# Value columns computed token by token in a mLSTM / SSD / retention step, and three changed orders on ScalarE and VectorE

## The reference, cut to what matters

```
p = rmsnorm(x) @ w_in
# layer 0: q, k, v, gates, og, z, xbc, dt = split(p)     mLSTM, 4 heads of 256 value columns, beside SSD
# layer 1: q, k, v, g = split(p)                         retention, 8 heads of 256 value columns
s = (q @ k^T) * decay ;  out = s @ v + (q @ state) ;  state = decay * state + (k * g)^T @ v
```

## Time and profile before

| | before |
|---|---|
| median of 3 runs | 1037.89 us (1037.03 to 1038.46) |
| the profiled execution, its own time | 1032.65 us |
| its span in the profile | 1030.9 us |
| TensorE busy, share of the span | 991.7 us, 96% |
| VectorE busy | 747.9 us, 73% |
| ScalarE busy | 559.2 us, 54% |
| GpSimd busy | 381.0 us, 37% |
| mean granted TensorE clock | 0.984 |

### The profile page before, as it was taken

The page is one execution under the profiler, slowest core; times in us unless marked ns, Lnnn a source line. Parts: engine busy times, 40 slices in busy tenths (PEclk is TensorE's granted clock), DMA queues, the critical chain, the costliest instruction groups (busy, mean ns, idle before and its releaser), DMA issues.

```text
span 1030.9 us, 19172 instructions
## 1 busy us (share of the span) xinstructions
PE 991.7 (96%) x7256; PEld 939.5 (91%) x7256; DVE 747.9 (73%) x1326; ACT 559.2 (54%) x932; POOL 381.0 (37%) x599
## 2 busy tenths in 40 slices
PE   7989999898899999999999999999999999999996
PEld 6989888777589999999999999899989999999996
DVE  5776788877866999996458857677765699999442
ACT  6536666633544766555444356666645566665431
POOL 4003223224211777772005521322222377777100
PEclk9999999999899999999999999999999999999998
DMA  8463464453555554545444735776635455544541
GB/s 295 140 242 123 129 210 131 153 187 108 168 180 185 173 175 165 164 164 180 163 164 164 266 126 189 219 236 183 206 133 187 161 172 170 169 166 165 179 144 46
DMA packets 64684, 177.22 MB, mean 172 GB/s; under 512 B 5888, under 2 KB 24064, under 8 KB 64592
## 3 DMA queue, kind: packets, MB, share of 16 engines
q1 hardware_dynamic: 64304, 174.86, 51.0%
q0 software_dynamic: 288, 1.12, 0.3%
HBM read 154.92 MB, written 21.05 MB: 171 GB/s over the span
## 4 chain that ended last, share of the span: by engine, by line
PE 85%; DVE 6%; ACT 4%; issue 3%; POOL 1%; DMA 1%; SPq 0%; DVEq 0%; ACTq 0%; POOLq 0%
PE bank L809 25%; PE bank L811 24%; PE bank L810 24%; PE bank L855 2%; ACT wh L1227 2%; DVE wl L1633 1%; PE bank L1165 1%; PE bank L1133 1%; DMA raw<-wts 1%; PE bank L1095 1%; PE bank L867 1%; POOL sts L2353 1%; PE bank L876 1%; PE bank L875 0%; PE bank L1139 0%
## 5 line engine op out<-in xcount | busy, mean ns | idle before, releaser
L1227 ACT ACTIVATE wh<-raw 128x1024 fp32r<-128x1024 f32 x257 | 270.5, 1057 | 318.3 <-PE bank L811 317.6
L1633 DVE TENSOR_TENSOR wl<-raw,wh 128x1024 fp32r<-128x1024 f32 x257 | 321.3, 1254 | 164.4 <-ACT wh L1227 162.4
L809 PE MATMUL bank<-hH,wh 128*128 128x288 f32 x1160 | 352.9, 304 | 7.1 <-DVE wl L1633 4.8
L810 PE MATMUL bank<-hL,wh 128*128 128x288 f32 x1160 | 345.5, 298 | 0.0
L811 PE MATMUL bank<-hH,wl 128*128 128x288 f32 x1160 | 344.3, 297 | 0.0
L809 PEld LDWEIGHTS bank<-hH,wh 128*128 128x128 f32 x1160 | 221.0, 191 | 10.7 <-DVE wl L1633 3.4
L810 PEld LDWEIGHTS bank<-hL,wh 128*128 128x128 f32 x1160 | 221.2, 191 | 0.6
L811 PEld LDWEIGHTS bank<-hH,wl 128*128 128x128 f32 x1160 | 221.5, 191 | 0.0
L1756 DVE SCALAR_TENSOR_TENSOR cy<-pad,vec,cy 128x304 f32<-128x304 f32 (+1 forms) x212 | 139.5, 659 | 4.5 <-ACT cy L1275 0.6
L2194 POOL COPY pad<-fst 128x16 f32<-128x16 f32 x88 | 94.3, 1076 | 67.7 <-DVE cy L1756 67.7
L809 PE MATMUL bank<-upH,wh 128*128 128x288 f32 x352 | 104.4, 297 | 0.0
(11 more groups left out here) (336 smaller groups left out, 1605.7 us busy)
## 6 DMA issues: line engine op xcount, KB each, us to landing
raw<-wts SPq DMA_DIRECT2D x257, 512.0 KB, 3.3
st<-r_in SPq DMA_DIRECT2D x9, 512.0 KB, 6.5
r_out<-st SPq DMA_DIRECT2D x9, 512.0 KB, 4.4
st<-c_in SPq DMA_DIRECT2D x8, 514.0 KB, 6.8
c_out<-st SPq DMA_DIRECT2D x8, 514.0 KB, 5.0
sts<-h_in SPq DMA_DIRECT2D x12, 256.0 KB, 5.1
h_out<-sts SPq DMA_DIRECT2D x12, 256.0 KB, 2.6
st3r<-r_in SPq DMA_DIRECT2D x4, 512.0 KB, 6.0
```

Source lines behind the costliest of these rows:

```text
L809: mm(out, h, xh, start=(k == 0), stop=False)
L810: mm(out, h, xl, start=False, stop=False)
L1227: s.do(act(wh[:, c % RING, :], raw[:, c % RING, :], ACT.Copy), hi_ready)
L1633: do(tt(wl[:, c % RING, :], raw[:, c % RING, :], wh[:, c % RING, :].bitcast(F32), ALU.subtract), lo_ready)
```

## The change

The change has two parts. The first gives the value columns another form. Two value tiles become one pair of 256 columns. The tokens are now stationary and the weights move: `value_half` issues, for each of eight K steps, six matmuls for the prompt (two blocks of 128 tokens, three products each, 256 weight columns moving) and two for the samples, whose high and low halves lie side by side as 64 stationary columns (`xsA`, `xsR`, made by ScalarE's `side_by_side`). The pair fills two tile banks, and TensorE claims both at its start. VectorE's `values` writes the token-major result directly, scaled by `rcol`, a column of inverse norms, which comes from one transpose of `rstd` per layer (`rc0`, `rc2`) and `row_columns`. The transposes of the value tiles and the copies behind them are gone. On the host, `ordered` puts the blocks of a pair in the order in which they are read.

The second changes three orders. `gate_exponentials` and `gate_slab` come two tiles later. ScalarE's `keys` comes before its step for tile t + 3, and before `inverse`, in both kinds of head. In the a-heads VectorE does the taps of tile t + 1 after the sample read-out and the updates, no longer before them.

```diff
@@ plan_banks, layer 1
         tile(group_tile(h, 0))
+        if turns_left:
+            tile(group_tile(h, 1))
         job(f"roi{h}", "act", "five")
...
@@ TensorE
+            def value_half(n, t, xs):
+                half, c = TILES[t][2] % 2, place(t, 0)[0]
+                if half == 0:
+                    claim(t)
+                    claim(t + 1)
+                    pe.wait_ge(xs_ready, n + 2)
+                out, smps, x = mb(t - half), mb(t - half + 1), operand_of(n)
+                pe.wait_ge(lo_ready, c + 1)
+                for i in range(4):
+                    k = 4 * half + i
+                    (xh, xl), w = x(k), slice(2 * i * P, 2 * (i + 1) * P)
+                    h, lo = wh[:, c % RING, w], wl[:, c % RING, w]
+                    for g in range(2):
+                        tok, to = slice(g * P, (g + 1) * P), out[:, g * AV:(g + 1) * AV]
+                        mm(to, xh[:, tok], h, start=(k == 0 and g == 0), stop=False)
+                        mm(to, xl[:, tok], h, start=False, stop=False)
+                        mm(to, xh[:, tok], lo, start=False, stop=(k == KD - 1 and g == 1))
+                    mm(smps[0:2 * NS, 0:AV], xs[:, k, :], h, start=(k == 0), stop=False)
+                    last = mm(smps[0:2 * NS, 0:AV], xs[:, k, :], lo, start=False, stop=(k == KD - 1))
+                last.then_inc(gemm_done, 1)
...
-                if t - 1 in VALUE:
-                    n = VALUE.index(t - 1)
-                    wait_tile_empty(pe, t - 1)
-                    turn(f"v{n}", vT[:, n % 2, :])
+                if t == RCOL["even"]:
+                    pe.wait_ge(rstd_ready, 1)
+                    turn("rc0", rstd)
@@ ScalarE
-                if t == GATES + 4:
+                if t == GATES + 6:
                     gate_exponentials()
...
                 product(f"asp{h}", pout[:, h % 2, 0:AV + 1])
-                step_a(t + 3)
                 if h + 1 < AH:
                     keys("a", h + 1, h + 1)
+                step_a(t + 3)
...
                     s.do(act(vst[row, 0:CV], rvA[0:NS, h, 2, :], ACT.Copy), vst_hi)
+                if h + 1 < CH:
+                    keys("r", h + 1, hg + 1)
                 step(h, 3)
                 if h:
                     inverse(hg - 1)
-                if h + 1 < CH:
-                    keys("r", h + 1, hg + 1)
@@ VectorE
+            def values(t, dst):
+                wait_tile(eng, t)
+                for g in range(2):
+                    do(ts(dst(g), mb(t - 1)[:, g * AV:(g + 1) * AV], rcol[:, g:g + 1], None, ALU.mult), gemm_dve if g else None)
+                b = mb(t)
+                do(ts(dst(2)[0:NS], b[NS:2 * NS, 0:AV], rcol[NS:2 * NS, 2:3], None, ALU.mult))
+                settle()
+                do(stt(out=dst(2)[0:NS], in0=b[0:NS, 0:AV], scalar=rcol[0:NS, 2:3], in1=dst(2)[0:NS],
+                       op0=ALU.mult, op1=ALU.add), gemm_dve)
...
-                if t == GATES + 5:
+                if t == GATES + 7:
                     gate_slab()
...
+                if t == RCOL["even"] + 1:
+                    row_columns("rc0")
...
-                step_a(t + 3)
+                step_a(t + 3, taps=False)
                 sample_out_a(h)
                 updates_a(h, range(4))
+                taps_of(t + 1)
```

More of the change, by code:

```diff
@@ L189, in plan_banks @@
             job("norm0", "act", "five")
[L190 to L191 removed]
+        if t == RCOL["even"]:
+            job("rc0", "dve", "five")
     for h in range(AH):
@@ L268, in plan_banks @@
             late_states(job, h - 1, "five")
-        tile(group_tile(h, 1))
-        if turns_left:
-            job(f"rv{2 * h + 2}", "dve", "five")
+        if not turns_left:
+            tile(group_tile(h, 1))
         job(f"ro1{h}", "act", "five")
@@ L297 @@
 GATES = START["even"] + EVEN.index(("gates", 0))
+RV = [START["odd"] + ODD.index(("rv", i)) for i in range(2 * CH)]
+RCOL = {"even": START["even"] + 5, "odd": START["odd"] + 4}
 def group_tile(h, step):
@@ L392, in build @@
         rstd = keep.take("rstd", [P, T])
+        rcol = keep.take("rcol", [P, 4])
         conv = Area(keep.at)
@@ L977, in _ @@
                     row_max(2)
-                tiles([t], operand_of(0))
+                if t in VALUE:
+                    value_half(0, t, xsA)
+                else:
+                    tiles([t], operand_of(0))
                 if t == T0 + 2:
@@ L1171, in group @@
                 t = group_tile(h, step)
-                if t < START["odd_out"]:
+                if t in RV:
+                    value_half(2, t, xsR)
+                elif t < START["odd_out"]:
                     tiles([t], operand_of(2))
@@ L1180, in _ @@
             for t in range(O + 2, O + LEAD):
-                tiles([t], operand_of(2))
+                if t in RV:
+                    value_half(2, t, xsR)
+                else:
+                    tiles([t], operand_of(2))
+                if t == RCOL["odd"]:
+                    pe.wait_ge(rstd_ready, 3)
+                    turn("rc2", rstd)
                 if t == O + LEAD - 2:
                     front("r", 0, qk_r)
-                    turn_value(0)
-            turn_value(1)
             for h in range(CH):
@@ L1275, in first_tap, with side_by_side @@
                 s.do(act(cy[:, n % 4, 0:width], x[:, 0:width], ACT.Identity, scale=tap, bias=bias), tap_done)
+            def side_by_side(n, xs):
+                eng.wait_ge(xlo_ready, KD * (n + 1))
+                for i in range(2):
+                    s.do(act(xs[:, :, i * NS:(i + 1) * NS], H[n][i][:, :, TP:T].bitcast(F32), ACT.Copy), xs_ready)
             def y_high(n, dst, src):
@@ L1575, in _ @@
                 split(last_chunk(t) + 3)
+                if t == O + 3:
+                    side_by_side(2, xsR)
             eng.wait_ge(rope_ready, 2 * CH)
@@ L1882, in _, with step_a @@
             eng.wait_ge(zeroed, 1)
-            def step_a(t):
+            def step_a(t, taps=True):
                 if t - 1 == GATES:
@@ L2088, in evacuate_odd @@
                 elif kind == "rv":
-                    scaled(t, rvT[:, i % 2, :])
+                    if i % 2:
+                        values(t, lambda g: rvA[:, i // 2, g, :])
                 else:
@@ L2119, in _ @@
                 split(last_chunk(t) + 3)
+                if t == RCOL["odd"] + 1:
+                    row_columns("rc2")
             front("r", 0, AH)
-            value(0)
             for h in range(CH):
@@ L2124, in _ @@
                 step(h, 0)
-                if h == 0:
-                    value(1)
-                else:
+                if h:
                     sample_out(h - 1)
@@ L2462, in halves, with ordered @@
         return weight_tiles(w).reshape(-1, 4, 2, CHUNK, P, P).swapaxes(1, 2).reshape(-1, P, P)
-    def ordered(w, tiles):
-        return weight_tiles(w).reshape(len(tiles), KD, P, P)[tiles].reshape(-1, P, P)
+    def ordered(w, tiles, values):
+        out = weight_tiles(w).reshape(len(tiles), KD, P, P)[tiles]
+        for n in values:
+            out[n:n + 2] = out[n:n + 2].swapaxes(0, 1).reshape(2, KD, P, P).copy()
+        return out.reshape(-1, P, P)
     odd_first = {"rq": 0, "rk": CH, "rv": 2 * CH, "rg": 4 * CH}
```

58 lines of the change are left out of this document (27 added, 31 removed).

## The result

The changed kernel takes 1057.9 us (median of 4 runs, 1057.68 to 1059.64) beside 1037.46 us for the kernel before: ratio 1.0206, 95% interval 1.0185 to 1.0227, or 20 us more. The forecast was 1049.3 us in a range of 1037 to 1060: the direction and the range held, and the size was 8.6 us short, so that the time lies above the 1043 to 1056 of the likeliest case. The profiled execution took 1059.64 us (span 1057.9).

What follows compares the result with a forecast made beforehand. TensorE was taken to bound from 345 to 540 us and in the r-heads, with waits and lower clock from 98 to 345 us. Terms 13.8 - 5.9 + 0 - 8 + 9 + 2.5 = +11.4 gave 1049.3 us, range 1037 to 1060.

Steps and rivals of the forecast that it cites:

- likeliest case: Whole kernel: the forecast sum holds, with its own range of 1043 to 1056 us; chance 0.62.
- Value matmuls, +13.8: Value tiles of both layers: a pair's K step goes from 0.800 to 0.944 us, +13.8 us over 12 pairs x 8 steps.
- load-bound rival: Value matmuls: each keeps 0.133 us because loading the stationary operand sets the pace; +23.2, 1061 us; chance 0.11.
- Transposes, -5.9: Value tiles: 24 value transposes go, less two new ones for `rc0` and `rc2`; -5.9 us.
- The whole value part, 7.9: Value tiles: the matmul term of +13.8 us and the transpose term of -5.9 us taken together.
- Gates, 0: Gates: two waits go, but a new 3.6 us wait at tile 9 for tile 7's bank comes; 0, bounds -3.5 and +2.
- A-heads, -8: A-heads: waits for `keys` and the read-out, with lower clock behind them, mostly go; -8 us, bounds -12 and -4.
- the prediction's own sign: A-heads: the prediction is wrong if they lose less than 4 or more than 12 us.
- R-heads, +9: R-heads 1 to 6: `back` newly waits 1.5 us each for VectorE's `normalise`; +9 us, bounds 0 and 11.
- Clock, +2.5: At the new waits: 1.5 losses of 1.7 us each to lower clock; +2.5 us, bounds 0 and 12.
- that the wait does not come: Rival, r-heads: ScalarE's late split is absorbed, so no new wait; +0.9, 1038.8 us; chance 0.17.
- The faster one: Rival, 98 to 345 us: relief of VectorE lets 22 us go, not 8; -2.6, 1035.3 us; chance 0.08.

Runs made afterwards that it cites:

- e3: The changed kernel with `keys` of the r-heads moved back behind the split and `inverse`; 1041.35 us, ratio 1.0062 to the kernel before.
- e10: The changed kernel with r-heads' `keys` behind `inverse`, `gate_logs` one tile later and `rcol` at the top of memory; 1035.09 us, ratio 1.0017 to the kernel before.
- e11: The kernel before with the changed orders of the gates and a-heads, taps moved last, no r-heads order or new value matmuls; 1025.38 us, ratio 0.9927.
- e6: The kernel before with the gates' order and a-heads' `keys` ahead of the split, taps left in place; 1026.12 us, ratio 0.9893.
- e4: The changed kernel with the taps of the a-heads back ahead of the split; 1059.03 us, ratio 1.0219 to the kernel before.
- e9: The changed kernel with `gate_logs` one tile later, behind the evacuation of tile 7; 1053.98 us, ratio 1.0216 to the kernel before.
- e5: The kernel before with only `rcol` allocated and never used, shifting tiles behind it by 32 bytes; 1038.60 us, ratio 1.0019.
- e7: The kernel before with the gates' order, a-heads' `keys` ahead of the split, and taps between read-out and updates; 1027.55 us, ratio 0.9916.

## Why the prediction was right in direction and short in size

*Value matmuls, +13.8.* Right. A K step takes 0.940 us in layer 0 and 0.947 in layer 1 (medians), so 32 x 0.140 + 64 x 0.147 = 13.9. The load-bound rival would have needed 1.06 us and is out. By the Trainium skill (TensorE: Matmul & The Clock Gate, "LDWEIGHTS (loading the stationary operand)") a load takes its number of columns / 1.2 in ns, an estimate of 107 ns for 128. The trace agrees in so far as such matmuls are 0.118 us apart, so a load can take no more of TensorE's time than that. Its records of the loads are longer, 0.188 us (median), and overlap one another; what of a record is the load itself no run here shows. The 64-column sample matmuls follow at 0.115 (57.25 to 57.36 to 57.48), as cheap as the others.

*Transposes, -5.9.* About right. In layer 1 the stage of e3 is 4.4 above that of before, with one low-clock stretch in each; 9.4 less 4.4 is 5.0 for its 16 transposes, where 14 x 0.24 + 2 x 0.33 = 4.0 was taken. The whole value part, 7.9, measured 9.3 to 9.7 between e10 and e11, with a wait of 1.6 us in it.

*Gates, 0.* The wait came at the tile forecast, with 3.75 us for 3.6. What was not in this term is the low clock: 6.8 us at half speed from 48.9 us on, of which the first 1.4 are still the wait, so that 2.7 us were lost. The waits that the order removes are worth 3 us where no pair of banks needs tile 7: tiles 8 to 21 take 3.0 less in e6 and 3.1 less in e11.

*A-heads, -8.* Too large by 4, and by the prediction's own sign (a loss of less than 4 us) wrong. The three waits for `keys` (4.1 us) and 1.7 us of the one for the read-out went, but the sum of waits did not: 6.5 us of waits for VectorE's `yF` and `st` took their place. From tile 21 to 38 TensorE idles 7.6 us, where it idled 7.9, and the clock rose only from 0.95 to 0.97. I gave back 4 where about 8 came back. VectorE is busy 80 of 96.7 us there, so I take it that VectorE sets the pace and that taking one wait away shows the next; e4 and e6 show other waits in the same stage, but no run made VectorE's work shorter. The 3.9 us gained are lower-clock time (some 1.9, from the record of the clock: 10.2 us at half speed before, 6.4 after), 0.3 of idle time, and a rest of 1.7 that the runs don't place.

*R-heads, +9.* Right: 1.4 us in each of six heads, 8.4, through the chain as forecast.

*Clock, +2.5.* This is the step that failed. I counted 1.5 losses over the new waits. The record has one long stretch at the wait of tile 9 (2.7 us lost) and six in the r-heads where before had one (8.0 us lost by e3): 10.7 in place of 2.5, inside the bounds of 0 to 12. The reason given for so few was that the new waits lie between work that fills the array. Around `back` that is not so: its own matmuls have 128 and 32 columns, and the products before it fill a part of the array (32*32 and 96*128 in the rows). Five of the six waits of 1.24 us were followed by a fall. Behind the 1.7 us at tile 9 in e9, between full tiles, there was none. That the small products make the difference is my reading; no run varied them alone.

*Not in the sum.* The unchanged stages lose 2.3 us through shifted operands, as e5 does.

Over the forecast, then: clock +8.2, a-heads +4.1, addresses +2.3, gates +0.3 (3.75 us of wait for 3.5 that went), matmuls +0.1, transposes -1.0, r-head wait -0.6, which is 13.4. The stages of the table, 24.4 measured and 11.0 forecast, say 13.4 too. With the 2.6 us outside those stages, for which 0.3 was forecast, the profiled execution was 15.5 above the 1044.1 forecast for it. Against the median it was 8.6, because the execution of before that I worked from lay 5.2 us below its median and that of after 1.7 above: 6.9 us of the smaller miss is the luck of the executions. It is luck too that the time lies in the stated range: 1057.9 is in the band of 1056 to 1064 that was kept for the load-bound rival, which did not hold.

Of the rivals, that the wait does not come was refuted by the rows, the load-bound one by the K step. The faster one needed 21.5 us or more back from the a-heads and the SSD part, and tiles 21 to 60 gave 3.9. Its objection, that the table gives the orders only 6.8 us of waits, was on the right side and still too kind: the idle time of the a-heads fell by 0.3.

## What to carry to other kernels

Before an instruction is moved ahead of a step that is ready earlier, list what is queued behind it on that engine and who waits for that: moving `keys` in the r-heads cost 15 to 16.5 us, more than both good orders gave (7 to 11 us). Price a new wait on TensorE for each of its repetitions, and look at what the clock may add: here 8.4 us of waits cost 8.0 us more by the clock. Don't add up the waits that an order takes away: of 5.8 us that went in the a-heads, 0.3 us of idle time came back. And test orders singly: the two that helped were hidden by the third.

## What the runs showed of the hardware that was not expected

- The distance between matmuls depends on where the operands lie. In tiles 62 to 89, 32 unused bytes per partition ahead of them turned 133.6 into 134.7 ns, and 64 bytes into 132.6 ns (86.16 us over the same tiles), 0.8% either way, the same to 0.01 us in e5 and the changed kernel. In tiles 114 to 133 the 64 bytes cost as much as the 32 (62.10 after 61.75 us). No run here says by what rule, or which operand it is.
- A wait of 1.24 us on TensorE, amid fp32 products, was followed by 3.4 us at a granted clock of 0.50 (2.4 down to 1.2 GHz) in five of six r-heads, 1.6 us lost each time. A wait of 1.7 us between full tiles (e9, tile 9) was not.
- A VectorE step that met `kgm` grew by about `kgm`'s own length: the taps by 1.96 us for 1.89. Moved clear of it (e7), they left the split to meet it, which grew from 1.22 to 2.89 us.
